# Mixture of experts on one core: skipped gather rows and a new row order for the expert weights

## What is computed

```python
TOP_K, N_EXPERTS = 8, 64          # EXPERT_FF = 256, D_MODEL = 1024, 512 tokens
_, top_idx = lax.top_k(sel, TOP_K)                 # 8 experts for each token
w = jnp.take_along_axis(scores, top_idx, axis=1)   # and a weight for each
...
def swiglu(x, w_gu, w_down):
    g, u = jnp.split(x @ w_gu, 2, axis=-1)         # (tokens, 1024) @ (1024, 512)
    return (jax.nn.silu(g) * u) @ w_down           # (tokens, 256) @ (256, 1024)
...
out = out.reshape(P, D) * buf_w[:, None]
routed = jnp.zeros((T + 1, D), x2d.dtype).at[buf_tok].add(out)[:T]
return routed + swiglu(x2d, w_sh_gu, w_sh_down)
```

## Time and profile before

| | us |
|---|---|
| median of 3 runs | 3598.62 (3589.8 to 3600.66) |
| the profiled execution | 3593.65 |
| its span | 3591.9 |
| TensorE's mean granted clock | 0.904 of full |

### The profile page before, as it was taken

How to read it: one execution, slowest core, us unless ns; L and a number is a source line. 1 busy time by engine, 2 the same in 40 slices (tenths; PEclk the granted TensorE clock), 3 DMA queues, 4 the chain that set the end, 5 groups by cost and what they waited for, 6 DMA issues and landing times.

```text
span 3591.9 us, 35820 instructions
## 1 busy us (share of the span) xinstructions
PE 2985.9 (83%) x11955; PEld 2109.1 (59%) x11955; DVE 2125.6 (59%) x3373; ACT 1368.0 (38%) x2065; POOL 188.0 (5%) x164
## 2 busy tenths in 40 slices
PE   6788989999989989999986755577876798888983
PEld 3344457788777768877663421145443677777773
DVE  1655544577629767762333428863231798888885
ACT  1332344222325542232222211133222577777773
POOL 0000000000000000000000000000000122222220
PEclk8788889999999999999897877789988899999997
DMA  2111012222231113323220000011302899999995
GB/s 78 47 47 40 31 47 94 94 94 93 65 111 47 47 55 98 98 72 92 71 70 0 24 6 0 23 47 45 108 27 108 293 359 359 360 364 360 359 363 173
DMA packets 290722, 437.43 MB, mean 122 GB/s; under 512 B 30043, under 2 KB 168723, under 8 KB 290611
## 3 DMA queue, kind: packets, MB, share of 16 engines
q1 hardware_dynamic: 270739, 363.68, 29.4%
q0 software_dynamic: 19872, 72.36, 7.4%
HBM read 395.10 MB, written 40.89 MB: 121 GB/s over the span
## 4 chain that ended last, share of the span: by engine, by line
PE 60%; SPq 16%; DVE 12%; ACT 4%; issue 4%; DMA 3%; DVEq 0%; ACTq 0%; PEldq 0%; POOLq 0%; PEld 0%
PE tp L955 36%; PE tp L914 12%; SPq L733 10%; SPq L740 5%; DVE uT L2462 1%; DMA ytab<-arena 1%; ACT arena L1429 1%; PE mp L974 1%; PE mp L1210 1%; PE mp L1195 1%; PE mp L988 1%; DMA arena<-in_a_in_proj 1%; DVE arena L2013 1%; PE mp L1134 1%; PE mp L1135 1%
## 5 line engine op out<-in xcount | busy, mean ns | idle before, releaser
L955 PE MATMUL tp<-sq_r,arena_r 128*128 128x512 f32 x1216 | 489.3, 402 | 36.0 <-DVE uT_r L1945 31.3
L955 PE MATMUL tp<-sq_r,wring_r 128*128 128x512 f32 x1216 | 484.4, 398 | 0.0
L955 PE MATMUL tp<-uT_r,arena_r 128*128 128x512 f32 x1216 | 483.6, 398 | 0.0
L955 PEld LDWEIGHTS tp<-sq_r,arena_r 128*128 128x128 f32 x1216 | 230.5, 190 | 101.0 <-issue 43.3
L955 PEld LDWEIGHTS tp<-uT_r,arena_r 128*128 128x128 f32 x1216 | 230.8, 190 | 58.3 <-issue 3.3
L955 PEld LDWEIGHTS tp<-sq_r,wring_r 128*128 128x128 f32 x1216 | 230.6, 190 | 53.8
L955 PE MATMUL tp<-arena_r,wring_r 128*128 128x512 f32 x608 | 243.4, 400 | 0.0
L1932 DVE TENSOR_TENSOR wring_r<-wring,arena_r 128x2048 fp32r<-128x2048 f32 x84 | 188.7, 2286 | 80.2 <-ACT arena_r L1442 80.1
L1429 ACT ACTIVATE raw<-tp 128x512 f32<-128x512 f32 x106 | 63.2, 597 | 448.8 <-PE tp L914 239.2
L914 PE MATMUL tp<-uT,wring 128*128 128x512 f32 x512 | 229.2, 610 | 0.0
L2013 DVE SCALAR_TENSOR_TENSOR arena<-raw,pcol,arena 128x512 f32<-128x512 f32 x272 | 204.5, 752 | 36.9 <-DVE arena L2013 8.6
(11 more groups left out here) (383 smaller groups left out, 5905.1 us busy)
## 6 DMA issues: line engine op xcount, KB each, us to landing
arena<-in_w_exp_down SPq DMA_DIRECT2D x64, 1024.0 KB, 18.3
wring<-in_w_exp_gu SPq DMA_DIRECT2D x64, 768.0 KB, 16.7
uT<-in_w_exp_gu SPq DMA_DIRECT2D x32, 768.0 KB, 17.1
sq<-in_w_exp_gu SPq DMA_DIRECT2D x32, 768.0 KB, 16.9
wring<-in_f_up_w SPq DMA_DIRECT2D x22, 1024.0 KB, 5.3
wring<-in_f_up_w SPq DMA_DIRECT2D x44, 512.0 KB, 6.6
wring<-in_w_exp_gu SPq DMA_DIRECT2D x32, 512.0 KB, 16.8
wring<-in_f_down_w SPq DMA_DIRECT2D x32, 448.0 KB, 5.4
```

What stands on the lines that cost most here:

```text
L955: ins = nc.tensor.matmul(b[:], parts[wp][:, kk, m * P:(m + 1) * P], xparts[xp][:, kk, :], start=n_k == 0 and q == 0, stop=n_k == k - 1 and ...
```

## The change

Three edits. (1) The gather gets a bounds check: an index above 511 is out of bounds, its row is skipped and the slot keeps what its buffer held. Empty slots have the indices 512 and up. The scatter is as before: it adds all 128 rows, the empty ones to the spare rows of `ytab`. (2) The weights are read so that partition p gets the neighbouring rows 8 p to 8 p + 7 of the first matrix, and 2 p and 2 p + 1 of the second. (3) Step k then holds the channels 8 p + k, so the transposes of the rows and of the activations read every 8th float (every 2nd for the activations) instead of 128 neighbouring ones.

```diff
@@ expert_gu @@
-                gu = pick(A["w_exp_gu_2"][0].rearrange("e (k p) n -> p e k n", p=P), e)
+                gu = pick(A["w_exp_gu_2"][0].rearrange("e (p k) n -> p e k n", p=P), e)
@@ expert_down @@
-                dn = pick(A["w_exp_down_2"][0].rearrange("e (k p) n -> p e k n", p=P), e)
+                dn = pick(A["w_exp_down_2"][0].rearrange("e (p k) n -> p e k n", p=P), e)
@@ m_gather @@
                 G.indirect_dma_start(out=xe[b], out_offset=None, in_=xtab,
-                                     in_offset=bass.IndirectOffsetOnAxis(ap=sidx[q], axis=0)).then_inc(gathered[b], 16)
+                                     in_offset=bass.IndirectOffsetOnAxis(ap=sidx[q], axis=0),
+                                     bounds_check=NTOK - 1, oob_is_err=False).then_inc(gathered[b], 16)
@@ m_turn @@
+                x = xe[b].rearrange("p (f k) -> p k f", k=NK)
                 for k in range(NK):
-                    ins = nc.tensor.transpose(tp[2 + k // 4][:, (k % 4) * P:(k % 4 + 1) * P], xe[b][:, k * P:(k + 1) * P], ident[:])
+                    ins = nc.tensor.transpose(tp[2 + k // 4][:, (k % 4) * P:(k % 4 + 1) * P], x[:, k, :], ident[:])
@@ m_actturn @@
+                a = actE.rearrange("p (f k) -> p k f", k=2)
                 for k in range(2):
-                    ins = nc.tensor.transpose(mp[0][:, k * P:(k + 1) * P], actE[:, k * P:(k + 1) * P], ident[:])
+                    ins = nc.tensor.transpose(mp[0][:, k * P:(k + 1) * P], a[:, k, :], ident[:])
```

## The result

The changed kernel takes 3611.3 us (median of 20 runs, 3600.0 to 3625.8), the kernel before 3597.4 us (20 runs): ratio 1.0039, 95% interval 1.0027 to 1.0050. It is 14 us slower, where 38 us less were forecast, and lies above the range. Its runs also scatter more, 26 us against 16 from the fastest to the slowest.

What follows compares the result with a forecast made beforehand. The prediction took the DMA engines to bound the expert loop. Longer runs save 0.60 of 11.62 us a period, 38 us over 64 experts, skip 0 and transposes hidden: 3598.6 - 38 = 3560 us, range 3512 to 3588.

Steps and rivals of the forecast that it cites:

- What bounds the kernel now: Expert loop, 64 experts at 11.62 us: full DMA engines set the pace and push back SyncE's weight issues.
- What is late next: Expert loop with weights early: VectorE has 10.24 us of work, so a period can't fall under 10.2 us.
- Longer runs: Weight reads: fewer packets at 12.6 ns fixed each save 9.6 us of engine time, 0.60 us a period, 38 us.
- Skipped rows: Gather: 64 of 128 rows skipped, 40 us if all engines are relieved alike, taken as 0.
- A2: Follow-up theory: skip empties the high slots' engines; the others' scatter meets more long weight packets; spreading gives 3560 to 3580 us.
- Strided transposes: TensorE, L1335 and L1354: ten a step at 0.055 us more each, 0.55 us a period, hidden under the DMA.
- Rival 4: L1335 and L1354: strided reads make TensorE the bound, slower, 3713 us at four times the interval; chance 7%.
- Rival 1: Gather: the skip relieves all 16 engines, 59 to 79 us less, 3520 to 3540 us; chance 23%.
- rival 2: Weight reads: long runs are cut at 4 KB or gain half, 19 us less, 3580 us; chance 14%.
- my four rivals: Rival 1, rival 2, Rival 4, and a third: new HBM addresses eat the gain, 3590 to 3605 us, chance 11%.
- The sum: Expert loop: 11.62 - 0.60 = 11.02 us a period, 38 us less over 64 experts, median 3560 us; chance 45%.

Runs made afterwards that it cites:

- skip_spread: Kernel before with the gather's bounds check and slots renumbered so that ranks 0 to 63 lie in partitions 0 to 31 and 64 to 95: 3566.7 us, ratio 0.9924.
- rows_only: Changed kernel without the bounds check, so new rows, long weight packets and strided transposes with all 128 rows gathered: 3582.6 us, ratio 0.9965 to the kernel before.
- rows_two: Changed kernel without the bounds check, with even and odd experts scattered to two tables summed at the end: 3579.2 us, ratio 0.9952 to the kernel before.
- the control: Kernel before with even and odd experts scattered to two tables summed at the end: 3601.3 us, ratio 1.0018.
- skip_only: Kernel before with the gather's bounds check alone: 3592.5 us, ratio 0.9988.
- short_runs: Changed kernel with first weights in 2 KB packets from the same new rows, second weights and their transposes as before: 3590.3 us, ratio 0.9984 to the kernel before.
- after_two: Changed kernel with even and odd experts scattered to two tables summed at the end: 3582.8 us, ratio 0.9964 to the kernel before.
- before_spread_sskip: Kernel before with the gather's bounds check, spread slots and the same bounds check on the scatter: 3531.9 us, ratio 0.9821.
- after_spread_sskip: Changed kernel with spread slots and the same bounds check on the scatter: 3542.0 us, ratio 0.9856 to the kernel before.
- after_spread: Changed kernel with ranks 0 to 63 spread over partitions 0 to 31 and 64 to 95: 3590.0 us, ratio 0.9982 to the kernel before.

## Why the prediction was wrong

**What bounds the kernel now** was right: weights behind full DMA engines. skip_spread, which only takes load off them, gains at once.

**What is late next** is the step that failed. I named VectorE (10.24 us), ScalarE and TensorE, all resources that are busy, and wrote that a period can't fall under 10.2 us. I did not name the chain of the scatters, which is busy nowhere: a landing of 9.1 us plus about 0.6 us until GpSimd issues the next (an estimate, from 12.1 us a step and 11.5 us of landing in the changed kernel) makes 9.7 us a period even in the kernel before, only 1.9 us below the bound. The row with the 9.1 stood in my own list, and I used it only to count experts. With 9.7 the chain would still have passed under VectorE's 10.24. What the sum put at nothing, without a reason, is what the change does to that landing: it rose to 10.6 us with the long packets (rows_only) and to 11.5 us with long packets and skip, a period of 12.1 us in that stretch where 11.02 were forecast.

**Longer runs.** Their effect on the engines' work had the right sign; the gain was mis-sized. rows_two gains 22 us on its control, 0.35 us an expert, 5.5 us of engine time, where 9.6 were forecast. The queue rows and the busy times of the two, 2900 to 3300 us, first the control, then rows_two, show where the rest went:
```profile
q1 hardware_dynamic: 46063, 107.73, 70.6%
...
2900.00:3300.00 400.00, 360.18 (x1745) 292.04 (x1745) 349.35 (x558) 291.78 (x417) 98.53 (x70) 0.98 1.05 361
...
q1 hardware_dynamic: 20279, 110.73, 67.3%
...
2900.00:3300.00 400.00, 370.02 (x1812) 300.50 (x1811) 363.86 (x580) 304.68 (x436) 102.06 (x72) 1.00 1.03 373
```
By the bytes these are 34.2 and 35.2 experts, so the weight packets of one expert took 132 us (70.6% of 16 x 400 us, over 34.2) and then 122 us: 9.5 us less, as forecast. But the DMA share, the overlap of packets on an engine, fell from 1.05 to 1.03 (by the two queues' shares from 104.5% to 103.0%), and 1.5% of the 187 us that an expert has on 16 engines are some 3 us of the 4 that are missing. The prices of the earlier trace rows came from stretches with shares of 1.05 and 1.04, and the forecast let that overlap stand. So the 12.6 ns a packet held for the time that packets take, and 5.5 us over the 768 packets saved, 7 ns each, is what came out as time; why long packets overlap less was not taken apart. What I left out weighs more: by turns, each of a scatter's 8 packets an engine waits for one weight packet. With the prediction's prices that is 8 x (308 + 84.8) = 3.1 us before, as the 3.1 us stretch shows, and 8 x (308 + 229) = 4.3 us with 6 KB, where 4.1 us were seen. That is 1.0 to 1.2 us of the 1.5 us by which the landing rises, to 10.6 us (rows_only). The period's floor is then some 11.2 us by the medians, and of the gain 13 us are left.

**Skipped rows.** Taking 0 for the skip was right (skip_only 4 us), and for the reason given: filled slots are the low ones, and the low and the high slots are on different engines (skip_only against skip_spread). The Trainium skill (DMA: Bandwidth & Descriptors, The descriptor swizzle) has slots 0 to 63 on one half of the engines; these two runs agree with it. What I took for free was not: with long packets the skip turned 13 us of gain into 14 us of loss. Through A2, spreading the slots takes 0.8 us off the landing and 21 us off the time. How exactly half-empty engines delay the full ones' scatter is argued, not shown: the weights' backlog then stands on one half alone, and each of the scatter's packets there meets a weight packet. Nor does the sum by turns carry over to the kernels with the skip: in skip_only the scatter's packets are spread over 4.4 us (median of the packet records, 238 weight packets beside them) where it was 3.1, and the scatter still lands in 8.9 us.

**Strided transposes** cost 2 to 3 ns each instead of 55, on a load that overlaps; short_runs, which has the eight of the rows, shows no loss from them. The rule on 16-byte lines (the Trainium skill, SBUF — State Buffer, Door 1) has a penalty for such reads; the load shows one, 141 to 194 ns, and the time none. Rival 4 was wrong. Rival 1 needed the spread slots, rival 2's 19 us is near the 22 us of rows_two by accident, since long packets were not cut (the packet records have 4, 6 and 8 KB). The loss came by none of my four rivals.

**The sum.** Of the forecast 38 us, the transfers gave 18 to 22 (after_two, rows_two), and the scatters' chain took 28 or more (changed kernel against after_two, which still carries the longer tail). Three readings behind the sum were also a little off: 11.62 us was one expert's step, while the scatters of the stretch are 11.5 us apart and those of the whole loop 11.31, so the loop is about 712 us and not 744, and the prices' 11.66 us agree with the stretch to 1.5% only; and the rate stands at 359 to 364 GB/s for seven slices, not eight.

## What to carry to other kernels

Beside each engine's busy time, add up every loop of transfer, wait and next issue, and compare its length with the period; and ask what the change does to each part of it; here a loop within a fifth of the bound (9.7 of 11.6 us) became the bound. Where two queues share the DMA engines by turns, longer packets on the one that streams make transfers on the other later: beside a dependent chain of scatters only 13 us of a forecast 38 came of them (rows_only), and with the skip short packets were the better choice (short_runs 3590 against 3611 us). And before rows are skipped, ask which engines they belong to: renumbering the slots gave more than the skip itself.

## What the runs showed of the hardware

A row skipped by the bounds check leaves a small packet (about 64 more under 512 B an expert), and the software queue carries as many packets as before. 768 weight packets fewer for the same bytes took 9.5 us less of the DMA engines' busy time, 12 ns each, and gave back 5.5 us of it as time, 7 ns each (rows_two against the control). Two queues with work took turns on the engines one packet for one, 128 scatter packets beside 121 to 132 of the weights. Reading a 128x128 transpose's operand with a stride of 32 bytes lengthened the load from 141 to 194 ns and the interval from 110 to 112 ns. And a scatter in which half of the rows are out of bounds landed in 8.6 us instead of 9.1 beside short weight packets (before_spread_sskip against skip_spread) and in 9.1 instead of 10.7 beside long ones (after_spread_sskip against after_spread): in the kernel before, the scatter's own packets fill only 3.1 us of its 9.1.
